# A new order of the work between two transformer blocks: the first row tile's normalisation sums queued ahead of a weight unit, its turns and the memory products reordered

## The reference, cut to what matters

```python
# end of the first block
    z = jnp.square(jax.nn.relu(h2 @ w_up[l]))
    x = x + (z @ w_down[l]).astype(x.dtype)      # "down", 4096 -> 1024
return rmsnorm(x, final_norm_g)
# start of the second block
    h = rms_norm(x, ln_mix_g[l])
    ... = jnp.split(h @ w_in[l], ...)            # "kvc", "small", "kv", "qa", ...
# memory attention of the second block: its keys and values need only the memory
    mem_n = rms_norm(mem, ln_mem_g[l])
    k, v = jnp.split(mem_n @ w_xkv, 2, axis=-1)  # "kx" and "vx"
```

## Time and profile before

| what | value |
|---|---|
| median of three runs | 863.0 us (862.0 to 869.16) |
| the profiled execution: its time | 865.17 us |
| the profiled execution: its span, first to last instruction | 863.4 us |
| mean granted TensorE clock | 0.990 |
| TensorE matmul busy | 827.2 us, 96% |
| TensorE weight load busy | 736.1 us, 85% |
| VectorE busy | 599.6 us, 69% |
| ScalarE busy | 454.0 us, 53% |
| SyncE's queue of loads | 137.11 MB |

### The profile page before, as it was taken

How to read it: one execution, slowest core, us unless ns; L and a number is a source line. 1 busy time by engine, 2 the same in 40 slices (tenths; PEclk the granted TensorE clock), 3 DMA queues, 4 the chain that set the end, 5 groups by cost and what they waited for, 6 DMA issues and landing times.

```text
span 863.4 us, 13091 instructions
## 1 busy us (share of the span) xinstructions
PE 827.2 (96%) x5359; PEld 736.1 (85%) x5359; DVE 599.6 (69%) x945; ACT 454.0 (53%) x798; POOL 95.7 (11%) x106
## 2 busy tenths in 40 slices
PE   6998999899999999999989899999998999999997
PEld 5876887689999888888987688999886999999885
DVE  5876667777666745558568686755768699999744
ACT  5755556446555634454575445652468554555433
POOL 4100000000000000000400000000000355555100
PEclk9999999999999999999999998999999999999999
DMA  9753644454665555473855333344643355555551
GB/s 313 225 179 118 197 134 153 138 171 154 237 195 179 180 181 193 145 244 105 245 176 166 98 98 98 99 138 151 210 159 100 117 177 194 191 169 180 194 195 49
DMA packets 85387, 143.47 MB, mean 166 GB/s; under 512 B 5026, under 2 KB 43200, under 8 KB 85328
## 3 DMA queue, kind: packets, MB, share of 16 engines
q1 hardware_dynamic: 83008, 137.11, 48.8%
q0 software_dynamic: 2160, 5.46, 2.2%
q10 hardware_dynamic: 160, 0.07, 0.0%
HBM read 141.05 MB, written 1.05 MB: 165 GB/s over the span
## 4 chain that ended last, share of the span: by engine, by line
PE 79%; DVE 12%; ACT 7%; issue 1%; DMA 1%; SPq 0%; DVEq 0%; ACTq 0%
PE PS L1204 77%; DVE low_r L2229 4%; PE PS L1213 2%; ACT high L1745 2%; ACT WK_f L1742 2%; DVE AR_f L2237 1%; DMA low_f<-in_w_in_dram 1%; ACT AR_f L1739 1%; DVE AR_f L2229 1%; DVE WK_f L2237 1%; DVE X L2229 1%; ACT HTh L1745 1%; DVE WK_f L2233 0%; DVE HTl_r L2229 0%; ACT L1739 0%
## 5 line engine op out<-in xcount | busy, mean ns | idle before, releaser
L2229 DVE TENSOR_TENSOR low_r<-low_f,high 128x1024 fp32r<-128x1024 f32 x254 | 324.4, 1322 | 85.8 <-ACT high L1745 85.6
L1745 ACT ACTIVATE high<-low_f 128x1024 fp32r<-128x1024 f32 (+1 forms) x262 | 256.9, 1030 | 81.5 <-DMA low_f<-in_w_down_dram 34.8
L1204 PE MATMUL PS<-HTh,high 128*128 128x256 f32 x888 | 254.9, 287 | 1.1 <-DVE HTl_r L2229 1.1
L1204 PE MATMUL PS<-HTl_r,high 128*128 128x256 f32 x888 | 252.3, 284 | 0.0
L1204 PE MATMUL PS<-HTh,low_r 128*128 128x256 f32 x856 | 243.3, 284 | 0.0
L1204 PE MATMUL PS<-high,AR_r 128*128 128x512 f32 (+1 forms) x656 | 193.0, 376 | 2.8 <-issue 1.9
L1204 PEld LDWEIGHTS PS<-HTh,high 128*128 128x128 f32 x888 | 171.1, 193 | 2.6 <-issue 2.3
L1204 PEld LDWEIGHTS PS<-HTl_r,high 128*128 128x128 f32 x888 | 171.0, 193 | 0.1
L1204 PEld LDWEIGHTS PS<-HTh,low_r 128*128 128x128 f32 x856 | 164.8, 192 | 0.0
L1204 PEld LDWEIGHTS PS<-high,AR_r 128*128 128x128 f32 (+1 forms) x656 | 116.5, 180 | 26.8 <-issue 3.0
L1204 PE MATMUL PS<-low_r,AR_r 128*128 128x512 f32 (+1 forms) x328 | 121.1, 373 | 0.0
(11 more groups left out here) (183 smaller groups left out, 854.3 us busy)
## 6 DMA issues: line engine op xcount, KB each, us to landing
low_f<-in_w_in_dram SPq DMA_DIRECT2D x40, 1024.0 KB, 5.2
low_f<-in_w_up_dram SPq DMA_DIRECT2D x38, 1024.0 KB, 5.2
low_f<-in_w_down_dram SPq DMA_DIRECT2D x27, 1024.0 KB, 4.9
low_f<-in_w_out_dram SPq DMA_DIRECT2D x8, 1024.0 KB, 5.1
low_f<-in_w_xkv_dram SPq DMA_DIRECT2D x4, 1024.0 KB, 5.4
low_f<-in_w_branch_gla_dram SPq DMA_DIRECT2D x2, 1024.0 KB, 5.1
low_f<-in_w_branch_nsa_dram SPq DMA_DIRECT2D x2, 1024.0 KB, 5.1
low_f<-in_w_xq_dram SPq DMA_DIRECT2D x2, 1024.0 KB, 5.3
```

Source lines behind the costliest of these rows:

```text
L1204: return nc.tensor.matmul(o, l, r, start=start, stop=stop, skip_group_check=True)
L1745: return nc.scalar.activation(o, i, ACT.Copy, bias=0.0, scale=1.0)
L2229: return nc.vector.tensor_tensor(o, a, b, op)
```

## The change

Two edits. The string of the order is replaced, and `rows` lists the pending low half of a unit after its very last step.

```diff
-TWO_NORMS = "M0M0MMM1M0M10MM1MM1M"
+TWO_NORMS = "000MMMM1M11MMM0M1M"
...
                 if i == 1:
                     self.done(self.U[key, 1, 1].full if q == 3 else None)
                     self.ahead(end + 2)
+                    if q == 3:
+                        self.lows()
                 yield
```

## The result

The changed kernel took 859.83 us in the median of 19 runs (857.86 to 865.6), the kernel before 863.24 us in 19 runs beside it (860.9 to 869.16): 3.4 us less. The ratio of the compared runs is 0.995, with a 95% interval of 0.9933 to 0.9967, so the kernel is faster by 0.3 to 0.7%, which is beyond the measurement's scatter, and less than the 1% that the prediction set as the bound of its classes. Forecast were 859.4 us and "same". The times of the kernel before lie in two groups, ten from 860.9 to 863.24 us and nine from 865.66 to 869.16 us, so its median stands at the edge of a gap; the means, 864.71 and 860.32 us, differ by 4.4.

What follows compares the result with a forecast made beforehand. TensorE was taken to bound the kernel (matmuls 96% of the span); removing its two waits, 1.3 + 2.3 = 3.6 us, took 863.0 to 859.4 us. Own range 858.3 to 861 (chance 0.68), wider range 857.0 to 863.2.

Steps and rivals of the forecast that it cites:

- same: Class for the whole kernel: within about 1%, 8.6 us, of no change; chance 0.96, faster 0.02, slower 0.02.
- Both waits: TensorE standing still between the blocks, 1.1 (1.3) us for lo59 and 2.1 (2.3) us for tile 0's scaled rows; both go.
- The sum: TensorE's waits between the blocks removed: 3.6 us by the weight loads' idle time (1.3 + 2.3), perhaps 3.8.
- The matmul row's 3.2: The same two TensorE waits counted by the matmuls' idle time, 1.1 + 2.1 us; not the figure taken.
- Scaling of tile 0: On VectorE, XN of tile 0 ready near 371.5 us instead of 389.7.
- Root of tile 1 waiting: ScalarE's root waits 1.6 us for inverses behind lo60; costed at nothing, at most 1.6 us.
- the first wait: TensorE's 1.1 (1.3) us before `kx` unit 59; goes because lo59's first half is 2.6 us early.
- the second's: TensorE's 2.1 (2.3) us before tile 0's turns; goes as they start at 389.0 with XN ready since 371.5.
- The clock rival: Low-clock stretch near 528 us changes by half: 1.7 us either way, 857.7 or 861.1 us; chance 0.12, half each way.
- Swallowed later: Rival: longer waits in the following attention take part or all of the gain, 861.7 or at most 863.0 us; chance 0.13.
- The stall of tile 1's turns: Rival: tile 1 scaled only at 398.66 us, TensorE stands 6.2 us, net 2.6 slower, 865.6 us; chance 0.04.
- No effect: Rival: ScalarE's squares of tile 0 don't start until hi58 is through, so nothing moves, 863.0 us; chance 0.03.

Runs made afterwards that it cites:

- experiment 1: Kernel before with only row tile 0's sums, inverses, root and scaling moved ahead of hi58; 861.5 us against 865.32, ratio 0.9946.
- Experiments 3: Changed kernel without its second edit, the added `lows`; 860.59 us against 865.32 for the kernel before, ratio 0.9937.
- experiment 4: Changed kernel with root and scaling of tile 1 moved to just ahead of tile 1's turns; 863.83 us against 865.32 for the kernel before, ratio 0.9985.

## Why the prediction was right

**What bounds, and why the waits.** Right. Both waits came from the squares of tile 0 behind hi58; experiment 1 undoes that alone and takes both.

**The sum.** 3.6 us by the weight loads' idle time; measured 3.65 by the read-out (27.85 - 24.20), 3.2 by the spans at the same clock (3.5 by their read-outs), 3.4 by the medians. The matmul row's 3.2 was too small for the stretch. On this the Trainium skill (Perfetto Trace Analysis, Identifying the Most-Contended Engine) pointed the right way, though it speaks of busy time as a measure of headroom and not of waits: the read-out sides with the weight loads' row. Started from the median, 859.4 was forecast and 859.83 measured. That these two are so close is partly luck: the median of the kernel before was 863.0 us in three runs, 863.24 in 19, 865.32 in 35 and 866.66 in 12, and the means of the first comparison differ by 4.4 us and not 3.4. What the experiments confirm is the 3.6 us in the stretch.

**The steps of the queues.** Scaling of tile 0: near 371.5 forecast, 370.98 to 371.73 measured. Additions of tile 1: 378.2 and 378.46. Lo59: 379.5 and 379.78. Root of tile 1 waiting: 1.6 and 1.71. Scaling of tile 1, end: 386.9 and 387.22. Low half of its turns: 398.6 and 398.66. `kvc`: 401.6 and 401.94. Of these some 0.24 us are an offset that stands in the trace ahead of any step of the change (VectorE's first addition of row tile 0: 365.46 us before, 365.70 after).

**Credit given to the wrong edits.** The prediction let the added `lows` stand for the first wait's going and the turns' new place for the second's. Experiments 3 and 1 show that neither was needed: with the additions of tile 1 free to start at 378.2, lo59 is early behind XN too, and XN of tile 0 is early for the turns in their old place. The sum was right as the root of both was one cause. Had I asked of each edit what happens without it, the working would have shown this.

**The clock rival.** Half right: the clock scatters, and the spans with it, by up to 5 us between executions of one program, without any shift. Whether the shift changes the clock besides is open (the 0.992 and 0.990 above). The prediction read one trace's low stretches as a property of the kernel and hung the rival on one of them, near 528 us. That the low stretches come and go between executions agrees with the Trainium skill (TensorE: Matmul & The Clock Gate, What's actually happening), by which the gate's check is free-running.

**The other rivals.** Swallowed later: no, 3.3 us ahead at `kvc` and 3.2 at the end. The stall of tile 1's turns: not there; experiment 4 shows that a late scaling is paid in full (3.3 of the 3.65 us), not the 6.2 us that the prediction reckoned for a still later one. No effect: the squares of row tile 0 start at 366.55 us, 8.5 us ahead of hi58.

## What to carry to other kernels

Where queues are served in order, look for work whose operands are ready and that stands behind an instruction that waits for a load: moved ahead into that idle time it costs nothing, and it pays as many microseconds as TensorE's own waits at the end of its chain, here two waits that looked separate and had one cause. Read that payment from start to start in one stretch, not from two spans, since a clock that falls in other places can add half as much again. Once the cause is gone, the exact places of the rest hardly matter here, until one is late; then the lateness counts in full.

## What the runs showed of the hardware that was not expected

Six executions of one program on one core, with the same instructions, had spans of 861.4 to 866.4 us at mean granted clocks of 0.987 to 0.993. After a wait of 2.1 us the clock stayed at its higher level in four of the six and fell in two, which made the following stretch 1.5 us longer (17.09 against 15.60 us). After 3.0 us of waiting some 5 us later in the program (experiment 4, one trace) it didn't fall.
